# TensorE's branch on overfull experts moved ahead of the last pack's second gate-up chunk, and layer 0's last down chunk loaded in two halves

## What is computed

```python
def hier_moe(h, w_group, w_router, w_gate_up, w_down):
    ...
    gu = jnp.einsum('td,edf->tef', hs, w_gate_up)
    act = jax.nn.silu(gu[..., :EXPERT_FF]) * gu[..., EXPERT_FF:] * gate[..., None]
    return jnp.einsum('tef,efd->td', act, w_down)
...
    for i in range(DEPTH):
        h = rmsnorm(x, norm_mix[i])
        ...
        x = x + jnp.concatenate([mix, xa], axis=-1) @ w_out
        x = x + hier_moe(rmsnorm(x, norm_ffn[i]), ...)
    return rmsnorm(x, final_norm), ...
```

## Time and profile before

| | us |
|---|---|
| median of three runs | 1155.56 (1155.17 to 1160.45) |
| the profiled execution | 1159.98 |
| its span in the trace | 1158.2 |
| outside the span (1159.98 - 1158.2) | 1.8 |
| TensorE busy | 1105.3 |
| VectorE busy | 509.8 |

### The profile page before, as it was taken

How to read it: one execution, slowest core, us unless ns; L and a number is a source line. 1 busy time by engine, 2 the same in 40 slices (tenths; PEclk the granted TensorE clock), 3 DMA queues, 4 the chain that set the end, 5 groups by cost and what they waited for, 6 DMA issues and landing times.

```text
span 1158.2 us, 17280 instructions
## 1 busy us (share of the span) xinstructions
PE 1105.3 (95%) x7354; PEld 753.0 (65%) x7354; DVE 509.8 (44%) x1089; ACT 172.0 (15%) x410; POOL 154.0 (13%) x103
## 2 busy tenths in 40 slices
PE   8999999999999999979999999999999999987895
PEld 7589996987574545436766757577699755433342
DVE  5446665633223232345444544644456333422234
ACT  2001113013111101020211112020200131100002
POOL 0000001510000000002431334240065100000000
PEclk9999999998999999989999999999999999999898
DMA  9973339835999999968445746486997369999994
GB/s 364 428 272 146 147 145 404 331 145 231 367 428 427 428 422 427 428 256 370 194 181 227 296 185 274 169 358 263 410 423 326 145 246 428 425 429 426 429 427 173
DMA packets 29904, 364.81 MB, mean 315 GB/s; under 512 B 3472, under 2 KB 3616, under 8 KB 7296
## 3 DMA queue, kind: packets, MB, share of 16 engines
q1 hardware_dynamic: 26928, 339.86, 71.3%
q10 hardware_dynamic: 1712, 19.17, 4.0%
q0 software_dynamic: 1184, 4.63, 1.0%
HBM read 339.32 MB, written 24.32 MB: 314 GB/s over the span
## 4 chain that ended last, share of the span: by engine, by line
PE 84%; DMA 13%; DVE 1%; issue 1%; ACT 0%; SPq 0%; DVEq 0%
DMA ring<-in_gu 10%; PE bank L1214 10%; PE bank L725 10%; PE bank L1150 9%; PE bank L910 7%; PE bank L1288 5%; PE bank L624 5%; PE bank L618 4%; PE bank L921 3%; PE bank L959 3%; PE bank L882 3%; PE bank L1123 3%; DMA ring<-in_dn 3%; PE bank L766 3%; PE bank L1207 2%; PE bank L683 1%
## 5 line engine op out<-in xcount | busy, mean ns | idle before, releaser
L910 PE MATMUL bank<-ring,arena 128*32 128x512 f32 x888 | 107.5, 620 | 22.0 <-DMA ring<-in_gu 20.7
L725 PE MATMUL bank<-arena,ring 128*128 128x144 f32 x896 | 110.4, 286 | 1.2 <-issue 1.2
L725 PEld LDWEIGHTS bank<-arena,ring 128*128 128x128 f32 x896 | 110.0, 190 | 1.4 <-issue 1.4
L910 PEld LDWEIGHTS bank<-ring,arena 128*32 128x32 f32 x888 | 28.0, 112 | 93.1 <-issue 69.9
L1949 DVE TENSOR_TENSOR xT<-xT,bank 128x288 f32<-128x288 f32 x128 | 58.1, 454 | 37.5 <-PE bank L959 33.8
L959 PE MATMUL bank<-arena 128*128 128x288 f32 x256 | 69.5, 414 | 3.2 <-issue 2.8
L959 PEld LDWEIGHTS bank<-arena 128*128 128x128 f32 x256 | 46.0, 190 | 25.8 <-issue 9.8
L1214 PEld LDWEIGHTS bank<-ring 128*128 128x128 f32 x448 | 56.2, 190 | 6.0 <-issue 6.0
L2416 POOL TENSOR_TENSOR ring<-ring 128x1024 f32<-128x1024 f32 x8 | 18.9, 2358 | 309.8 <-DVE arena L2276 309.7
L882 PE MATMUL bank<-arena 128*128 128x256 f32 x256 | 59.5, 386 | 0.0
L1214 PE MATMUL bank<-ring 128*128 128x144 f32 x448 | 58.2, 287 | 0.0
(11 more groups left out here) (331 smaller groups left out, 1599.7 us busy)
## 6 DMA issues: line engine op xcount, KB each, us to landing
ring<-in_gu SPq DMA_DIRECT2D x55, 2048.0 KB, 21.4
ring<-in_dn SPq DMA_DIRECT2D x28, 2048.0 KB, 20.2
ring<-in_rin SPq DMA_DIRECT2D x14, 2048.0 KB, 13.6
ring<-in_cin SPq DMA_DIRECT2D x8, 2048.0 KB, 27.5
ring<-in_kc SPq DMA_DIRECT2D x8, 2048.0 KB, 10.0
ring<-in_vc SPq DMA_DIRECT2D x8, 2048.0 KB, 8.9
ring<-in_st SPq DMA_DIRECT2D x8, 2048.0 KB, 8.7
out_rs<-ring ACTq DMA_DIRECT2D x8, 2048.0 KB, 7.2
```

The source lines that it names most:

```text
L725: mm = pe.matmul(out[:, o, :], w[:, o, k, :], x[:, k, :], start=(first and o == 0 and k == 0), stop=(k == 3), skip_group_check=True)
L910: mm = pe.matmul(bank[2][32 * e:32 * e + 32, :], xt[:, k, 32 * e:32 * e + 32], w[2 * e + kk], start=(k == 0), stop=(k == KD - 1), skip_gro ...
```

## The change

TensorE's program for the last pack goes into a function of its own, `last_pack`, from chunk 1 on. The branch stands behind chunk 0. Its first side (overfull experts) holds the last pack and then the extra passes; its other side, `Else`, holds the last pack alone. So the last pack is written twice, and with no overfull expert TensorE jumps over the first side, and runs the second. Both layers now use `last_pack` and `last_quarters`: layer 0's last down chunk comes in two loads of 1 MB and is multiplied in two halves, `keep_warm(1)` and `keep_warm(2)` stand behind the turned gates and activations in layer 0 too, and in layer 1 three `keep_warm` matmuls stand ahead of chunk 0 instead of four. ScalarE copies the last 256 columns (`last_rows_out`) in layer 0 as well, ahead of its squares for the next norm, and VectorE copies 256 columns instead of 512. The semaphore counts follow (`YSUMS`, `YOUTS`, `16 * (L + 1)`). The branches of the other engines stay.

```diff
+YSUMS, YOUTS = 2 * PACKS + 1, PACKS + 1
...
-                elif name == RING[-1]:
+                elif name in SPILL_AT:
                     sp.dma_start(slot(n % R)[:, 0:half], src[:, 0:half]).then_inc(S("last_half"), 16)
...
                 def last_quarters():
...
-                    pe.wait_ge(S("last_half"), 16)
-                    down_quarter(0, slot(AT[RING[-1]] % R)).then_inc(S("y_sum"), 1)
-                    down_quarter(1, landed(pe, RING[-1])).then_inc(S("y_sum"), 1)
+                    last = ("dn", (L, i, 1))
+                    pe.wait_ge(S("last_half"), 16 * (L + 1))
+                    down_quarter(0, slot(AT[last] % R)).then_inc(S("y_sum"), 1)
+                    down_quarter(1, landed(pe, last)).then_inc(S("y_sum"), 1)
                     combine(i, (4, 5))
...
+                def last_pack():
+
+                    i = PACKS - 1
+                    for c in range(1, 4):
+                        if c == 2:
+                            pe.wait_ge(S("xt_out_d"), PACKS * L + i + 1)
+                            combine(i - 1, range(0, 5))
+                        if c == 3:
+                            combine(i - 1, range(5, KD))
+                            if L == 0:
+                                keep_warm(3)
+                        gate_up_chunk(c, gate_up_landed(L, i, c), xgT).then_inc(S("gu_sum"), 1)
+                    pe.wait_ge(S("gated"), PACKS * L + i + 1)
+                    pe.wait_ge(S("gt_out"), PACKS * L + i)
+                    turn_gates().then_inc(S("gt_turned"), 1)
+                    keep_warm(1)
+                    pe.wait_ge(S("act_ready"), PACKS * L + i + 1)
+                    turn_act().then_inc(S("act_turned"), 1)
+                    keep_warm(2)
+                    pe.wait_ge(S("actT_out"), PACKS * L + i + 1)
+                    down_half(0, down_landed(L, i, 0)).then_inc(S("y_sum"), 1)
+                    combine(i, range(4))
+                    last_quarters()
...
                     if i == PACKS - 1 and L == 1:
-                        keep_warm(4)
-                    for c in range(4):
+                        keep_warm(3)
+                    for c in range(1 if i == PACKS - 1 else 4):
...
+                    if i == PACKS - 1:
+                        break
...
                 with pe.If(more > 0):
+                    last_pack()
                     pe.wait_ge(S("y_added"), KD * PACKS * L + KD * PACKS)
...
+                with pe.Else():
+                    last_pack()
...
+            def last_rows_out(L):
+
+                act.wait_ge(S("y_sum"), YSUMS * L + YSUMS)
+                act.activation(yo[:, 768:1024], bank[5][:, 0:256], ACT.Copy).then_inc(S("y_out_a"), 1)
```

More of the change, by code:

```diff
@@ L337, in wait_used @@
                 l, i, part = c
-                eng.wait_ge(S("gu_sum" if k == "gu" else "y_sum"), (4 if k == "gu" else 2) * (PACKS * l + i) + part + 1)
+                if k == "gu":
+                    eng.wait_ge(S("gu_sum"), 4 * (PACKS * l + i) + part + 1)
+                else:
+                    eng.wait_ge(S("y_sum"), YSUMS * l + 2 * i + part + 1 + (name in SPILL_AT))
                 return
@@ L987, in combine @@
                             pe.wait_ge(S("y_out_d"), PACKS * L + i + 1)
-                        if o == 6 and L == 1 and i == PACKS - 1:
-                            pe.wait_ge(S("y_out_a"), 2 * PACKS + 1)
+                        if o == 6 and i == PACKS - 1:
+                            pe.wait_ge(S("y_out_a"), YOUTS * L + YOUTS)
                         if o == 1 and i != PACKS - 2:
@@ L998, in last_quarters @@
                     i = PACKS - 1
[L999 to L1001 removed]
+                    last = ("dn", (L, i, 1))
+                    pe.wait_ge(S("last_half"), 16 * (L + 1))
+                    down_quarter(0, slot(AT[last] % R)).then_inc(S("y_sum"), 1)
+                    down_quarter(1, landed(pe, last)).then_inc(S("y_sum"), 1)
                     combine(i, (4, 5))
[L1003 to L1004 removed]
+                    if L == 1:
+                        pe.wait_ge(S("squares_added"), 6)
+                        final_sums((0,), "squared", KD * NORM["final"])
                     combine(i, (6, 7))
[L1006 removed]
+                    if L == 1:
+                        final_sums(range(4, KD), "squared", KD * NORM["final"]).then_inc(S("final_sum"), 1)
+                def last_pack():
[20 more added lines that the diff above has]
+                    last_quarters()
                 pe.wait_ge(S("htok_scaled"), 3 * (L + 1))
@@ L1020, in experts @@
                     if i == PACKS - 1 and L == 1:
-                        keep_warm(4)
-                    for c in range(4):
+                        keep_warm(3)
+                    for c in range(1 if i == PACKS - 1 else 4):
                         if c == 2:
                             pe.wait_ge(S("xt_out_d"), PACKS * L + i + 1)
-                        if c == 2 and i == PACKS - 1:
-                            combine(i - 1, range(0, 5))
-                        if c == 3 and i == PACKS - 1:
-                            combine(i - 1, range(5, KD))
-                            if L == 0:
-                                keep_warm(3)
                         gate_up_chunk(c, gate_up_landed(L, i, c), xgT).then_inc(S("gu_sum"), 1)
+                    if i == PACKS - 1:
+                        break
                     if i == 0:
                         count_chosen()
-                    if i + 1 < PACKS:
-                        pick(i + 1)
+                    pick(i + 1)
                     if i == 0:
@@ L1049, in experts @@
                     turn_gates().then_inc(S("gt_turned"), 1)
-                    if i == PACKS - 1 and L == 1:
-                        keep_warm(1)
                     if L == 0 and i in MEMORY_IN:
@@ L1055, in experts @@
                     turn_act().then_inc(S("act_turned"), 1)
-                    if i == PACKS - 1 and L == 1:
-                        keep_warm(2)
-                    if i and i < PACKS - 1:
+                    if i:
                         combine(i - 1)
-                    if i + 1 < PACKS:
-                        turn_x(i + 1)
+                    turn_x(i + 1)
                     pe.wait_ge(S("actT_out"), PACKS * L + i + 1)
                     for n in range(2):
-                        if i == PACKS - 1 and L == 1 and n == 1:
-                            last_quarters()
-                            break
                         down_half(n, down_landed(L, i, n)).then_inc(S("y_sum"), 1)
-                        if i == PACKS - 1:
-                            combine(i, range(4 * n, 4 * n + 4))
                 with pe.If(more > 0):
+                    last_pack()
                     pe.wait_ge(S("y_added"), KD * PACKS * L + KD * PACKS)
@@ L1584, in experts @@
                         turned_out(i + 1)
-                    act.wait_ge(S("y_sum"), 2 * PACKS * L + 2 * i + 1)
+                    act.wait_ge(S("y_sum"), YSUMS * L + 2 * i + 1)
                     act.activation(yo[:, 0:512], bank[5][:, :], ACT.Copy).then_inc(S("y_out_a"), 1)
-                if L == 1:
+                if L == 0:
+                    last_rows_out(0)
+                else:
                     act.activation(idle, G("eps")[0:1, :], ACT.Sqrt)
@@ L2011, in experts @@
                         ins.then_inc(S("squares_added"), 1)
-                    dve.wait_ge(S("y_sum"), 2 * PACKS * L + 2 * i + 2)
-                    if i == PACKS - 1 and L == 1:
+                    dve.wait_ge(S("y_sum"), YSUMS * L + 2 * i + 2)
+                    if i == PACKS - 1:
                         dve.tensor_copy(yo[:, 512:768], bank[6][:, 0:256]).then_inc(S("y_out_d"), 1)
```

10 lines of the change are left out of this document (3 added, 7 removed).

## The result

The changed kernel took 1161.32 us in the median (1158.87 to 1165.29, 20 runs) where the kernel before took 1157.11 (1155.17 to 1161.73, 20 runs) on the same chip. The ratio is 1.0032, 95% interval 1.0022 to 1.0042: slower by 0.3%, inside the half per cent that was called the same. The forecast was +1.4 us; the two comparisons say +2.2 and +3.7.

A forecast was written before the change was run, and what follows sets the result against it. TensorE, busy 95% of the span, was taken to bound the kernel. Layer 0's -1.15 (5.75 lost, 6.9 gained) and layer 1's +2.6 made +1.4 on 1155.56: 1157.0 us, range 1149.8 to 1165.0.

The forecast's parts named there:

- The price of the branch: Branch behind chunk 0, both layers: fetches its target's block under DMA load, 6.4 us from start to end, bounds 3.8 and 9.7.
- The fast fetch: Rival: the branch's fetch is as fast as on an idle DMA, 3.77 us; total -5.7, 1149.9 us; chance 0.13.
- the target at hand: Rival: the branch's target is already fetched, 0.35 us or less; total -6.9, 1148.7 us; chance 0.07.
- the slow fetch: Rival: the branch's fetch waits as long as the packet at 494.1, 9.7 us; total +8.0, 1163.6 us; chance 0.2.
- the fetch of blocks in order: Rival: the jumped-over block is fetched first, so two fetches, 10.9 us; total +10.4, 1166.0 us; chance 0.1.
- The extra of 2.6 us: Branch in the pack: added fetch time because DMA engines are full of weights, taken nearest to an 8 KB store's delay.
- The half clock: TensorE's clock drops after the branch's idle time in the pack: 1.9 us lost in layer 0, 1.7 in layer 1.
- (a): Layer 0's first down chunk: keep-warm matmuls fill the waits ahead, so it takes 1.92 us: -1.47.
- (b): End of layer 0: last down chunk in halves, first half's copy runs under the second half's matmuls: -0.87 us.
- (c): End of layer 0, branch gone: the wait ahead of the projection is 0.9 us instead of 3.03: -2.1.
- (d): Projection behind layer 0: clock stays full, first 32 rows take 8.4 us instead of 10.88: -2.5.
- the start of the branch: Layer 1's last pack: branch starts at about 1117.8, ahead of chunk 0 at 1119.3, as only three keep-warm matmuls stand ahead.

The follow-up runs named there:

- the two comparisons: The changed kernel against the kernel before, measured twice, unchanged: 1161.32 us against 1157.11 (ratio 1.0032), later 1160.68 against 1158.29 (1.0019).
- e1_cut: Kernel before with two of four gate-up chunks left out of layer 0's never-run extra passes, 64 instructions fewer: 1154.15 us against 1159.42, ratio 0.9953.
- e6_next: e2_end plus a second branch in layer 0's last pack, behind chunk 0, over 84 never-run matmuls (337 instructions): 1157.41 us, ratio 0.9987 to before.
- e7_longidle: Kernel before with 100 never-run matmuls added to layer 0's extra passes, so its end branch jumps 723 instructions: 1156.63 us, ratio 0.9991.
- e11_short: Changed kernel, but the branch behind chunk 0 jumps only 9 instructions; extra passes have their own branch at the end: 1154.33 us, ratio 0.9958 to before.
- e4_l1mid: Changed kernel with only layer 1's branch in the pack, layer 0's back at the end: 1165.77 us, ratio 1.0052 to before.
- e3_l0mid: Changed kernel with only layer 0's branch in the pack, layer 1's back at the end: 1157.08 us, ratio 0.998 to before.
- e2_end: Changed kernel with both branches back behind the last pack; halves, keep-warm matmuls and ScalarE's copy stay: 1155.97 us, ratio 0.9973 to before.
- e10_cutend: e2_end with three of four gate-up chunks and one of two down chunks left out of layer 0's extra passes: 1152.66 us, ratio 0.995 to before.
- e8_pad: e2_end plus 100 already-met semaphore waits at TensorE's program start, layer 0's last-pack keep-warm matmuls cut in three: 1155.14 us against before's 1158.29, ratio 0.997.

## Why the prediction was right in kind and short in size

**The price of the branch** was forecast at 6.4 us in both layers; it is 6.17 and 6.38. The reading behind it (a block fetched by the branch, 3.77 on an idle DMA and more under load) is what e1_cut, e6_next, e7_longidle and e11_short show. The fast fetch, the target at hand, the slow fetch and the fetch of blocks in order fall by the four durations of the changed kernel, the last by e7_longidle too. The extra of 2.6 us taken from the 8 KB store was near the mark (6.2 in e6_next less 3.4 in e7_longidle is 2.8). The other row that it was weighed against, the packet at 494.1, gave the upper bound of 9.7. Its reading, that the block is entered in the chunk at 486.89, holds with e4_l1mid's boundary (6,598, some 31 entries behind the place of the change's branch, 6,567); with the packets' boundary it is entered up to 20 entries later, in the spread matmuls. And the lateness is not steady: in e7_longidle, the same code up to there, the packet starts at 490.2, 4.1 us behind that chunk's start, for 7.1 in before. Seven branches under load took 6.03 to 6.51 us, so no waiting branch met the longer delay; why it came in before stays open.

**Layer 0: forecast -1.15, the profile shows -2.4.** Counted from chunk 0's start to the end of the projection's first 32 rows, it was 43.18 us before (484.18 to 516.48 + 10.88) and is 40.77 (483.22 to 515.99 + 8.00).
- Chunk 1 starts 6.30 us behind chunk 0 and not 2.71, 3.6 late for a forecast of 4.2. The branch started with chunk 0 (483.3 for 483.22), not half a microsecond behind it, and took 0.2 less.
- The cover of 0.35 was used up: no wait for weights is left ahead of chunk 2.
- The half clock cost 0.92 in chunk 1 and 0.74 in the spread matmuls, 1.7 for 1.9.
- (a), (b) and (c) together: from chunk 3 to the projection it was 19.23 and is 14.91, -4.3 for a forecast of -4.4. The wait is 1.04 for the 0.9 of (c).
- (d): 8.00 for 10.88, -2.9 for -2.5; the 8.4 scaled from eight rows was a little high.

**Layer 1: forecast +2.6, the profile shows +4.5.** From the start of the keep-warm matmuls to chunk 3 it was 14.13 us and is 18.62. The cover went as said (no wait for weights is left where there were 0.21 and 1.33), and the price was right. **The term that failed is the start of the branch.** It was put 0.6 us behind the keep-warm matmuls, on the argument that only these stand ahead of chunk 0 and that the sequencer runs ahead. It started at 1114.5, 2.1 behind them, with chunk 0's first matmul: +1.5. The sequencer had run 2.8 us ahead for the load of the pass count, but not for a branch behind chunk 0: in both layers, and in e11_short (487.1 with a chunk at 486.98), it started when chunk 0 did. Why it waits for the chunk no run tells. The half clock cost 2.1 for 1.7 (3.64 and 3.06 for 1.92 and 2.69), the other +0.4.

**The sum.** The two places give -2.4 + 4.5 = +2.1 us in the profiles; the ratios say +3.7 and +2.2 us. Layer 0 was forecast 1.25 us too high and layer 1 1.9 too low, so that the sum was only 0.7 off by the profiles: the mechanism was right, that the two errors nearly cancelled was luck. The changed kernel differs from e3_l0mid in layer 1's branch alone; by their ratios (1.0032 and 1.0019, less 0.998) that branch costs 6.0 or 4.5 us, which agrees with a loss in layer 1 well over the forecast 2.6. e3_l0mid, with layer 0's part alone, agrees in both views (-2.3 in the stretch and in the median). The difference between 1157.0 and 1161.32 has one more part, which is no term: the median of three runs of before that the forecast started from, 1155.56, was 1157.11 with twenty.

**What a profile pair can't carry.** Two of the gains are not in every execution. The first down chunk took 3.39 us at half clock in before's profile and 1.92 in that of e7_longidle, which runs the same code up to there, so (a) is worth 1.5 us in some executions and nothing in others. The 32 rows behind a wait of 2.62 us took 8.00 in e2_end and 9.46 in e7_longidle. This is why most of the kernels with a gain in layer 0 gained less in the median than in the stretch: e10_cutend's stretch is 35.92 (484.82 to 520.74), 7.3 less than before's, its median 5.7 less. That the sizes match is argued, not shown, and so is what makes up the 1.6 us between the profiles' +2.1 and the +3.7 of the first comparison.

**What it means for the change.** The halves and the keep-warm matmuls gain; moving the branch into the pack, where the DMA engines are full, loses more. With nothing left out, e11_short (0.9958) and e2_end (0.9973) beat both kernels. What would bring e10_cutend's 0.995 is shorter code for the extra passes, or an end of the layer about a hundred entries later in the program at no cost in time; both tries at the latter paid for it elsewhere.

## What to carry to other kernels

A jump over code that doesn't run is priced by where its target lies, so count both ends in the engine's program before moving a branch: within what has been fetched it costs 0.2 to 0.4 us, beyond it a fetch of 3.3 to 4.0 us, and 6.0 to 6.5 us where the DMA engines are full of weights. Put such a jump where nothing waits behind it (the end of layer 1: 3.3 to 4.0 us without effect) or shorten what it jumps over; cover by waits elsewhere in the pack is small (0.35 and 1.54 us here) and goes first. And code that never runs is not free where it pushes a target out of reach: 64 instructions fewer of it gave 5.3 us of 1159, more than the scheduling of the change gave by itself (e2_end, 3.1 by its ratio).

## What the runs showed of the hardware that was not expected

- A fetch under load waits before its packet, not in it: the packet of 16 KB came 3.6 to 4.0 us after the branch began, with the 16 engines full (seven branches), and 1.0 us after in before, e2_end and e7_longidle, with the engines idle or nearly so.
- A target near the end of its block stalls twice. In e4_l1mid 6.03 us for the branch were followed, 20 entries on, by 2.06 us more, and by a clock of 0.50 and 0.53 up to 1136.8 us. The kernel was 9.8 us over e2_end, where the traces of the changed kernel, whose target lay elsewhere in its block, gave 4.5 for the same move.
- A branch behind a chunk of matmuls began with the first of them, not ahead of it (1114.5 and 1114.46 in layer 1, and within 0.1 us in all nine of these branches), though a register load further up ran 2.8 us ahead.
- A wait for a semaphore that is already up is not free on TensorE: 100 of them in a row, two to an instruction, ran from 2.6 to about 7.9 us in e8_pad, 0.11 us an instruction, and put the first matmul 2.4 us back.
- Small fp32 matmuls, each with its weight load, don't scale down: 384 columns took 0.35 us (2.10 for 6), the same in three of 128 took 0.36, and in six of 64 took 0.69 (4.13 for 36).
